# A two-layer decoder trunk on one core: GpSimd powers instead of ScalarE roots in the last norm, and an expert's last chunk ordered by output halves

## What is computed

```python
def rmsnorm(x, g):
    xf = x.astype(jnp.float32)
    xf = xf * lax.rsqrt(jnp.mean(xf * xf, axis=-1, keepdims=True) + EPS)
    return (xf * g.astype(jnp.float32)).astype(x.dtype)
...
    for e in range(N_EXPERTS):
        out = out + combine[:, e:e + 1].astype(t.dtype) * swiglu(t, w_gate[e], w_up[e], w_down[e])
...
        x = x + rmsnorm(f, norm_g[i, 3])
        gate = jax.nn.sigmoid(rmsnorm(x, norm_g[i, 4]) @ ple_w_gate[i])
        x = x + rmsnorm(gate * (p[i] @ ple_w_proj[i]), norm_g[i, 5])
```

## Time and profile before

| | us |
|---|---|
| median of 3 runs | 1730.58 |
| lowest and highest run | 1730.53, 1732.64 |
| profiled execution | 1728.74 |
| its span, first to last instruction | 1727.1 |
| TensorE busy | 1699.8 (98%) |
| VectorE busy | 1502.3 (87%) |
| ScalarE busy | 1284.4 (74%) |
| GpSimd busy | 119.3 (7%) |

### The profile page before, as it was taken

The page is one execution under the profiler, slowest core; times in us unless marked ns, Lnnn a source line. Parts: engine busy times, 40 slices in busy tenths (PEclk is TensorE's granted clock), DMA queues, the critical chain, the costliest instruction groups (busy, mean ns, idle before and its releaser), DMA issues.

```text
span 1727.1 us, 27394 instructions
## 1 busy us (share of the span) xinstructions
PE 1699.8 (98%) x9279; PEld 1506.4 (87%) x9279; DVE 1502.3 (87%) x1978; ACT 1284.4 (74%) x1747; POOL 119.3 (7%) x143
## 2 busy tenths in 40 slices
PE   8999999999999999999999999999999999999997
PEld 7998889999889988887888888888888888888886
DVE  6898668888579896679999999989999999999997
ACT  6757747444467668468888888898888888888886
POOL 1210000000011300002001000010010100103200
PEclk9999999999999999999999999999999999999999
DMA  9764556555666845647999999999999999999992
GB/s 297 224 200 149 191 193 194 188 195 195 241 172 212 246 155 181 204 165 281 403 409 408 400 402 404 392 406 401 392 404 400 398 404 390 409 399 400 404 359 93
DMA packets 206268, 516.39 MB, mean 299 GB/s; under 512 B 10738, under 2 KB 73076, under 8 KB 206196
## 3 DMA queue, kind: packets, MB, share of 16 engines
q1 hardware_dynamic: 198768, 493.81, 77.6%
q0 software_dynamic: 7104, 21.54, 3.9%
q10 hardware_dynamic: 324, 0.12, 0.0%
HBM read 503.35 MB, written 7.88 MB: 296 GB/s over the span
## 4 chain that ended last, share of the span: by engine, by line
PE 91%; DVE 4%; ACT 2%; issue 1%; DMA 1%; SPq 0%; DVEq 0%; ACTq 0%; POOL 0%
PE bank L1991 68%; PE bank L2004 9%; PE bank L2039 5%; PE bank L2041 2%; PE bank L2535 1%; DVE wlo L1233 1%; DMA raw<-in_moe_w_gate_dram 1%; PE bank L2164 1%; ACT whi L720 0%; DVE U L1361 0%; PE bank L2190 0%; PE bank L2545 0%; PE bank L2180 0%; PE bank L2118 0%; PE bank L2177 0%
## 5 line engine op out<-in xcount | busy, mean ns | idle before, releaser
L1233 DVE TENSOR_TENSOR wlo<-raw,whi 128x1024 fp32r<-128x1024 f32 x880 | 1026.9, 1222 | 104.7 <-ACT whi L720 104.2
L720 ACT ACTIVATE whi<-raw 128x1024 fp32r<-128x1024 f32 x880 | 915.3, 1055 | 256.2 <-PE bank L1991 192.9
L1991 PE MATMUL bank<-whi,XGH 128*128 128x512 f32 x896 | 343.2, 383 | 1.0 <-DVE wlo L1233 1.0
L1991 PE MATMUL bank<-wlo,XGH 128*128 128x512 f32 x896 | 339.6, 379 | 0.0
L1991 PE MATMUL bank<-whi,XGL 128*128 128x512 f32 x896 | 339.6, 379 | 0.0
L1991 PEld LDWEIGHTS bank<-whi,XGH 128*128 128x128 f32 x896 | 169.4, 189 | 25.0 <-DVE wlo L1233 1.8
L1991 PEld LDWEIGHTS bank<-whi,XGL 128*128 128x128 f32 x896 | 169.3, 189 | 24.0
L1991 PEld LDWEIGHTS bank<-wlo,XGH 128*128 128x128 f32 x896 | 169.5, 189 | 22.8
L2004 PE MATMUL bank<-HHL,whi 128*128 128x256 f32 x1056 | 180.4, 277 | 0.0
L1991 PE MATMUL bank<-whi,ATH 128*128 128x512 f32 x448 | 172.5, 385 | 0.0
L1991 PE MATMUL bank<-wlo,ATH 128*128 128x512 f32 x448 | 169.8, 379 | 0.0
(11 more groups left out here) (366 smaller groups left out, 2231.9 us busy)
## 6 DMA issues: line engine op xcount, KB each, us to landing
raw<-in_moe_w_gate_dram SPq DMA_DIRECT2D x112, 1024.0 KB, 7.7
raw<-in_moe_w_up_dram SPq DMA_DIRECT2D x112, 1024.0 KB, 8.4
raw<-in_moe_w_down_dram SPq DMA_DIRECT2D x112, 1024.0 KB, 7.4
raw<-in_w_in_dram SPq DMA_DIRECT2D x56, 1024.0 KB, 5.9
raw<-in_ffn_w_gate_dram SPq DMA_DIRECT2D x14, 1024.0 KB, 5.0
raw<-in_ffn_w_up_dram SPq DMA_DIRECT2D x14, 1024.0 KB, 5.0
raw<-in_ffn_w_down_dram SPq DMA_DIRECT2D x14, 1024.0 KB, 5.0
raw<-in_w_proj_a_dram SPq DMA_DIRECT2D x8, 1024.0 KB, 5.1
```

The source lines that it names most:

```text
L720: nc.scalar.activation(whi[b % SPL][:, r], raw[b % RAW][:, r], ACT.Copy).then_inc(s_hi, 1)
L1233: v.tensor_tensor(wlo[b % SPL][:, r], raw[b % RAW][:, r], whi[b % SPL][:, r].bitcast(F32), ALU.subtract).then_inc(s_lo, 1)
L1991: ins = mm(dst, a, turns(b), start=start and n == 0, stop=stop and n == 2, skip_group_check=True)
```

## The change

In the last norm of layer 1 the table load, the two roots and the two inversions are gone. GpSimd takes both powers, behind its last gain row. VectorE sums block 0 ahead of block 1's third quarter, adds block 0's first half ahead of the last quarter's product and its second half behind the last partial sum. The square of the last quarter moves from VectorE to ScalarE, behind its last sigmoid.

In an expert's last chunk (d = 13) TensorE finishes bank 4 before bank 5, and tells it with a new semaphore `m_yh`; ScalarE evicts bank 4 on that and bank 5 on `s_pe`. The wait for `s_lo` now stands before every three matmuls of all 14 down chunks.

```diff
@@ pool
             gain_row(GROW[5], 1, 5, s_g)
+            for b in range(BLK):
+                power_z(5, b)
@@ scalar, job
                     if c == FFN - 1:
-                        act.wait_ge(s_pe, 2 * (MOE0 + FFN) + 2 * FFN * j)
                         act.wait_ge(m_yd, 16 * j + 32)
                         act.wait_ge(m_nx, j + 1)
                         for h in range(2):
+                            if h:
+                                act.wait_ge(s_pe, 2 * (MOE0 + FFN) + 2 * FFN * j)
+                            else:
+                                act.wait_ge(m_yh, j + 1)
                             nc.scalar.activation(by_halves(Y[:, half(h)]), straight(B[4 + h]), ACT.Copy,
@@ scalar, end
             gate_part(1, jobs, 1)
-            table(ACT.Sqrt)
-            root_z(5, 0)
-            root_z(5, 1)
+            act.wait_ge(s_zp, pcount(5, 1, 1) + 1)
+            act.wait_ge(*squared[-1])
+            nc.scalar.activation(SQJ[:, 0:256], Z[1][:, 1, part(1)], ACT.Square, accum_out=LAST[:, 0:1]).then_inc(s_zd, 1)
@@ vector, embedded_part
-                else:
-                    v.tensor_tensor_reduce(SQR[layer][:, :], z, z, 1.0, 0.0, ALU.mult, ALU.add,
-                                           LAST[:, 0:1]).then_inc(s_zd, 1)
-                    if n == 2:
-                        mean_last(n)
+                elif layer == 0:
+                    v.tensor_tensor_reduce(SQR[:, :], z, z, 1.0, 0.0, ALU.mult, ALU.add, LAST[:, 0:1]).then_inc(s_zd, 1)
+                    mean_last(n)
@@ vector, end
             embedded(1, 0, 0)
             gain_z(5, 0, 0)
-            bias_z(5, 0)
             embedded(1, 1, 0)
             gain_z(5, 1, 0)
             embedded(1, 0, 1)
             gain_z(5, 0, 1)
+            mean_z(5, 0).then_inc(s_zb, 1)
             embedded_part(1, 0)
             bias_last(5)
+            inverse_z(5, 0)
+            add_half(5, 0, 0)
             embedded_part(1, 1)
-            add_z(5, 0)
+            mean_last(5)
+            add_half(5, 0, 1)
             add_z(5, 1)
@@ tensor, down chunks
-                        for k in range(2):
+                        for n in range(4):
+                            k, h = (n // 2, n % 2) if d < 13 else (n % 2, n // 2)
                             split(b, k, j)
-                            for h in range(2):
-                                ins = three_turned(B[4 + h][:, :], wslot(b), (ATH, ATL),
-                                                   (A, slice(D * k + 512 * h, D * k + 512 * h + 512)),
-                                                   (A, 2 * d + k, A), d == 0 and k == 0, d == 13 and k == 1)
-                            ins.then_inc(s_pe, 1)
+                            ins = three_turned(B[4 + h][:, :], wslot(b), (ATH, ATL),
+                                               (A, slice(D * k + 512 * h, D * k + 512 * h + 512)),
+                                               (A, 2 * d + k, A), d == 0 and k == 0, d == 13 and k == 1)
+                            if h:
+                                ins.then_inc(s_pe, 1)
+                            elif d == 13 and k:
+                                ins.then_inc(m_yh, 1)
```

More of the change, by code:

```diff
@@ L182, in bass_hybrid_rglru_diffattn_moe @@
         ZGB = {2: at("ZGB2", o_q + 16 * KB, [P, D]), 5: at("ZGB5", o_sga, [P, D])}
-        SQR = (at("SQR0", o_q + 20 * KB, [P, 256]), at("SQR1", o_sga + 4 * KB, [P, 256]))
+        SQR = at("SQR", o_q + 20 * KB, [P, 256])
         Z = (at("Z0", o_q, [P, BLK, D]), at("Z1", a0 + 16 * KB, [P, BLK, D]))
@@ L363, in bass_hybrid_rglru_diffattn_moe @@
         m_yd = sem("m_yd")
+        m_yh = sem("m_yh")
         m_no = sem("m_no")
@@ L753, in root_z @@
                 act.wait_ge(s_zb, 2 * n + b + 1)
-                halved = n in (2, 5) and b == 1
-                if halved:
-                    act.wait_ge(s_zd, n // 3 + 1)
-                else:
-                    act.wait_ge(s_zq, zcount(n, b, 1))
-                nc.scalar.activation(stat(DZ, b), LAST[:, 0:1] if halved else ssz(b, 1), ACT.Sqrt, bias=stat(BZ, b),
+                act.wait_ge(s_zq, zcount(n, b, 1))
+                nc.scalar.activation(stat(DZ, b), ssz(b, 1), ACT.Sqrt, bias=stat(BZ, b),
                                      scale=1.0 / D).then_inc(s_zs, 1)
@@ L1270, in bias_last @@
             def bias_last(n):
[L1272 to L1275, removed]
+                by_power[1] = mark(mean_z(n, 1))
             def mean_last(n):
@@ L1323, in inverse_z @@
                 dve.wait_ge(s_zs, 2 * n + b + 1)
-                if n not in (0, 2):
+                if n not in (0, 2, 5):
                     link(v.reciprocal(stat(RZ, b), stat(DZ, b)))
```

## The result

| | before | after |
|---|---|---|
| median, us | 1730.01 | 1734.93 |
| lowest and highest run | 1728.65, 1732.64 | 1733.87, 1736.62 |
| profiled execution, its span | 1728.74, 1727.1 | 1735.41, 1733.4 |

The ratio is 1.0027, 95% interval 1.0018 to 1.0036. The forecast was 1729.9 with a range up to 1732.2, so the changed kernel is 5 us slower than forecast. It is 4.9 us slower than the kernel before, where 0.7 less was forecast.

What follows compares the result with a forecast made beforehand. In the experts' stretch the matrix engine was the bound, busy 903.84 of 905.00 us. Gains of 0.62 (end) and 0.11 (last expert), 0.7 us, took the median from 1730.58 to 1729.9 us; range 1727.9 to 1732.2.

Steps and rivals of the forecast that it cites:

- The end: Layer 1's last norm: GpSimd's second power is held until VectorE's addition ends, and VectorE's end comes 0.62 us earlier.
- Rival 1: Last norm: GpSimd's power isn't held up by VectorE, gain 1.06 us in all, 1729.5 us; chance 35%.
- rival 3: Last norm: the reordering eats the gain through late powers and an uncovered sigmoid, 1730.8 us; chance 8%.
- The sum: Whole kernel: 0.62 us at the end plus 0.11 at the last expert, 0.7 us gained, median 1729.9 us.
- The last expert: Between last expert and tail: first scatter load, released by an earlier eviction, hides behind filling matmuls; gain 0.11 us, bounds 0 and 0.25.
- Rival 5: Last expert's eviction stays behind the conversion, so no gain there, 1730.0 us; no chance given.
- The seven boundaries and the 224 waits: Expert boundaries and down projections: TensorE waits at no boundary, 28 more waits per expert cost under 1 ns each; cost 0.
- rival 4: Experts' down projections: added waits on a register cost time, 1741.1 us at 50 ns each; chance 3%.
- The last expert's stall: Last expert: TensorE's 1.8 us wait for wlo may change by up to 0.6 us either way; taken as 0.
- rival 2: Last expert: the stall moves with the gather, 1729.3 or 1730.5 us; chance 15% each way; sign, wlo wait differing from 1.8 us.
- The 4% left over: Experts' stretch: a disturbance of the experts' DMA or code fetch, to which no row speaks; chance 4%.
- worst case within the costs: Whole kernel: slow end of the range before the spread of runs was added, 1731.1 us.

Runs made afterwards that it cites:

- e3: The kernel before with one wait added at the end of GpSimd's program, for VectorE's last addition to X; 1736.28 us, ratio 1.004.
- e4: The changed kernel with an explicit drain on GpSimd behind its last gain row, ahead of the two powers; 1729.3 us, ratio 0.9998.
- k2: The kernel before, unchanged, run once more for a second profiled execution; 1729.93 us.
- g2: The changed kernel with the early drain behind GpSimd's last gain row, run once more; 1729.51 us, ratio 0.9999.

## Why the prediction was wrong

**The end.** Right: the order, the power held behind the addition, the second half of block 0 as its cover. That the sum came out to 0.01 us is partly luck, since the steps on the way were off by up to 0.04 us either way (the last sum 2.08 behind the last matmul by forecast, 2.05 measured; the second product 1.01 and 1.05). Rival 1 (power not held up) fell; of rival 3 nothing came.

**The sum: this step failed.** It put the path behind GpSimd's last power at nothing. It took the 0.62 us by which VectorE's last addition came earlier for a gain of the whole program, as if only the output's DMA stood between the two. It asked what waits for GpSimd's powers (block 1's additions), and not what stands behind them on GpSimd's own queue. That was GpSimd's drain at the program's end, 9.43 us long in the trace of before, and it lay 20 us clear of the end only because GpSimd's last work was at 1697. Moving a 0.55 us instruction to 1723 moved these 9 us with it. Once one takes it that the drain follows GpSimd's last instruction, as e3 then showed, the missing term can be worked out from the trace of before: power over at 22.60 on the scale of the forecast, drain 9.43 - 0.59 = 8.84 behind it, 1731.4, against SyncE's 1726.9 less 0.62, 1726.3: 5.1 us more, and -0.7 for the rest, 4.4 in all; measured 4.9 between medians, with 1.6 either way by the interval. e3 (a wait alone, 6.7 us) and e4 (an early drain, all of it back) show that nothing else is needed.

**The last expert.** Right: 31.39 to 31.41 us from the last expert's last matmul to the program's in every kernel that has the experts' part of the change, 31.51 to 31.53 in those without. Rival 5 fell: after the change the eviction starts at 1689.18, ahead of the last matmul's start at 1689.37.

**The seven boundaries and the 224 waits.** Right: no period changed. Of the named cases that end slower than before, rival 3 (1730.8) and rival 4, neither came; the cause that did was not among them.

**The last expert's stall.** The bound of 0.6 us either way was too narrow: with unchanged code the expert's length moves by 0.8 between executions, by 1.3 up to the kernel after, and the time ahead of it by up to 4. The sign named for rival 2, a wait for `wlo` other than 1.8 us, doesn't tell it from chance: it was 2.5 after the change, and 2.6 in k2 and e3, where that part is unchanged.

**Chances.** 0.93 for no change had everything in it that was on the path before the change. The 4% left over were given to the experts' DMA and code fetch; the end of the program was not among them. The range had a slip as well: its worst case within the costs, 1731.1, leaves out rival 3 together with the stall, 1730.8 + 0.6 = 1731.4. The measured 1734.93 lies outside either.

**A version that beats both?** The kernel after with an early drain has the forecast gain in its trace (span 1726.9, VectorE's end 4.74 us behind the last matmul, a last drain of 1.1 us), and with both additions behind the sum another 0.28. Against before the medians give 0.9998 and 0.9998 (g2 0.9999), intervals 0.9989 to 1.0008: some 5 us better than the changed kernel, not to be told from before.

## What to carry to other kernels

Ask of each engine what it still owes behind its last instruction, and look at the queues' closing instructions in the trace: an engine that ended early can carry a long closing piece that nobody sees. When GpSimd has issued DMAs, don't give it late work without a drain of its own behind the last of them, placed where GpSimd idles for as long as that drain takes; count 0.08 us per DMA, and the landing of those still under way. And a gain at the last instruction of one engine is one of the program only if the other engines' ends move too or have room.

## What the runs showed of the hardware

- A drain of GpSimd takes 0.082 us for each DMA that GpSimd has issued since its last drain, also when they landed a millisecond ago: 0.38 us behind 4, 8.8 behind 107. The other engines' drains at the end of the kernel after were over with their last instructions (SyncE 13 ns, ScalarE 0.54 us, VectorE 1.45, TensorE 2.31).
- A drain waits as well for GpSimd's DMAs that are under way (3.7 to 4.9 us behind a gain row, 7.2 to 7.4 behind the write of `Y`, 512 KB each).
- A power of one column takes 0.55 us alone, 0.66 to 0.68 when it starts inside a 128x256 product of VectorE, and 0.99 to 1.01 inside a 128x512 addition; each time it is over 0.40 to 0.43 behind the end of that instruction. Beside a VectorE product that reads a bank (layer 0, 258.91 and 265.17 in the trace of before) it takes 0.57 and 0.55 and isn't held.
- Two profiles of one kernel differed by 4 us in their span, while medians of such runs agree to 0.2.
